# Two transformer blocks on one Trainium2 core: x, the memory tokens, p and the norm weights come feature-major from the host

## The chip, the cores and the metric

The kernel runs on one core of a Trainium2 chip. The metric is the device time of one execution in microseconds. Lower is better.

## The reference

The input x is a float32 sequence of 256 tokens with 2048 features. It goes through a first block of two layers and a second block of one layer. Almost all of the work is products of the 256 tokens with float32 weight matrices; the rest is norms, attention and gates.

```python
# first block, layer 0 (pool) and layer 1 (latent attention)
xn = rms_norm(h, pre_norm[i])
out = pool_mixer(xn, ...) if i == 0 else mla_mixer(xn, ...)
h = h + rms_norm(out, post_norm[i])
gate = sigmoid(rms_norm(h, ple_norm[i]) @ ple_w_gate[i])
h = h + (p[i] @ ple_w_proj[i]) * gate          # p[i]: 256 tokens x 256

# pool_mixer begins with the largest product: 2048 -> 2 * 4096
z = xn @ w_in

# second block: a mixer, cross attention to 256 memory tokens, a feed-forward part
k, v = split(rms_norm(mem, mem_norm) @ w_kv, 2)
```

`rms_norm(x, g)` is x / sqrt(mean(x²) + eps) · g. The weights g are constants of the features; the mean is one number of each token.

## The kernel before, in words

Every engine runs its own hand-written program, and semaphores order them. TensorE contracts over the partitions, so the left operand of a product has to lie feature-major: 128 features on the partitions, 256 tokens along the row, 16 such k-tiles for 2048 features. Tensors that are token-major (`h`, `ptok` for p, `memt` for the memory tokens) are turned by TensorE with an identity matrix, a bank of PSUM for two k-tiles (`to_bank`, L563), and read from the bank by ScalarE and VectorE.

Float32 values are split into a high and a low part: ScalarE writes the high part (`xpose_hi`, L993 or L990: a copy that rounds, times the norm weight, which is one number of each partition), VectorE the remainder (`xpose_lo`, L1375 or L1370). A product is then three matmuls, high·high, low·high, high·low (L598 to L600). The norm's factor 1/rms of each token is multiplied in later, when ScalarE reads the product out of PSUM (`read_out`, L1033).

The weights stream through the core in **units** of 512 KB: two k-tiles by 512 columns. SyncE loads a unit into one of 8 slots of `raw` (L446), ScalarE writes `w_hi` (L968, function `hi`), VectorE writes `w_lo` (L1346, function `lo`), both into rings of 4 slots, and TensorE does 12 matmuls with it. A slot of `raw` is loaded again when its `w_lo` is there; a slot of `w_hi` is written again when TensorE is done with it. I call the units 0, 1, 2, 3 and so on. ScalarE and VectorE are kept three units ahead (`LEAD`): they split units 0 to 2 among the pieces of x, then everything that belongs to the norm of x, and only behind it, in the first loop, unit 3.

At the start SyncE loads the identity, 7 small rows of norm weights, `h` (x, 2 MB, token-major), the band matrix and then the units. GpSimd loads positions, the other norm weights (one row of 128 values on each partition), a mask and p. The norm weights go through TensorE too (`gain_columns`, L649 and L1053). TensorE turns x; at the same time GpSimd squares `h` (L1873), VectorE adds the squares up (L1434, `x_sums`), takes the mean (L1397) and ScalarE the root (`root`, L1028). ScalarE stops at the end of its start part until VectorE has the reciprocal (L1402), since the readings of the loop need it:

```python
root(0)
act.wait_ge(S("rstd0"), 1)
with act.Fori(0, WB) as g, ...        # hi(unit 3) is the first thing in here
```

VectorE does the angles of the rotary embedding (L1412 to L1426) as the first thing of all.

p is turned once for each layer of the first block, shortly before it is used (`xpose(ptok, 2)`): for layer 0 ahead of the product with `yh` and `yl`, for layer 1 right behind attention. The memory tokens are turned piece by piece while their first product runs (`first_chunk`): three pieces of two k-tiles ahead, then one piece after each of the first five units. In that product ScalarE does for each unit a `hi`, a square of `memt` for the norm, and the high part of a piece; VectorE does a `lo` and the low part.

Of the kernel before, what the change touches and what calls it, by code (L numbers as in the profile page):

```python
# [25 lines left out]
D = 2048  # L26
# [42 lines left out]
GAIN_TILES = [  # L69
    [("pre0", 16), ("pre1", 16), ("ple0", 16), ("ple1", 16), ("pool_scale", 32), ("q_norm", 4), ("kv_norm", 4), ("mix", 16)],  # L70
    [("cross", 16), ("ffn", 16), ("mem", 16), ("conv_b", 43)],
    [("conv_w0", 43), ("conv_w1", 43)],
    [("conv_w2", 43)],
]
GAIN = {name: 128 * t + sum(n for _, n in tile[:k]) for t, tile in enumerate(GAIN_TILES) for k, (name, _) in enumerate(tile)}

# [53 lines left out]
class Tally:  # L130


    def __init__(self):
        self.n, self.reg, self.per = {}, None, {}
# [28 lines left out]
def build(nc, a, out):  # L163
# [31 lines left out]
    gain = fixed("gain_columns", [128, 512])  # L195
# [16 lines left out]
    rows = arena("gain_rows", 32768, [128, 4, 128])  # L212
# [16 lines left out]
    ptok = arena("ple_tokens", 116736, [128, 2, 256])  # L229
# [38 lines left out]
    memt = arena("mem_tokens", 32768, [128, 2, D])  # L268
    kvm = arena("mem_kv", KVM, [128, 2, 1024])
# [118 lines left out]
    def heads_done(eng, before):  # L388
# [3 lines left out]
    vectors = {"pre0": a["pre_norm"][0], "pre1": a["pre_norm"][1], "ple0": a["ple_norm"][0], "ple1": a["ple_norm"][1],  # L392
               "pool_scale": a["pool_scale"][0], "q_norm": a["mla_q_norm"][0], "kv_norm": a["mla_kv_norm"][0],
               "mix": a["norm_mix_2"][0], "cross": a["norm_cross_2"][0], "ffn": a["norm_ffn_2"][0],
               "mem": a["mem_norm_2"], "conv_b": a["conv_b_2"][0], "conv_w0": a["conv_w_2"][0, 0],
               "conv_w1": a["conv_w_2"][0, 1], "conv_w2": a["conv_w_2"][0, 2]}

    def load_gains(eng, tiles, sem):

        for n in tiles:  # L400
            at_row = 0
            for name, r in GAIN_TILES[n]:
                eng.dma_start(rows[at_row:at_row + r, n, :], vectors[name].rearrange("(r c) -> r c", c=128)).then_inc(S(sem), 16)
                at_row += r

# [29 lines left out]
    def _(sp):  # L435
# [109 lines left out]
    def _(pe):  # L545
# [96 lines left out]

        pe.wait_ge(S("ident_in"), 16)

        def gain_columns(tiles):
            b = take_bank()
            for n in tiles:
                r = sum(x for _, x in GAIN_TILES[n])
                last = pe.transpose(TB(b)[:, n * 128:n * 128 + r], rows[0:r, n, :], ident[0:r, 0:r])  # L649
            last.then_inc(S("t_full"), 1)  # L650
# [39 lines left out]
        pe.wait_ge(S("ple_in0"), 16)  # L690
        xpose(ptok, 2)
        ready_ple = last_banks(1)
# [120 lines left out]
        attention([MLA], "ukv")  # L813
        pe.wait_ge(S("ple_in1"), 16)
        xpose(ptok, 2)
        ready_ple = last_banks(1)
# [1131 lines left out]
```

## Time and profile before

| | us |
|---|---|
| median of 3 runs | 2696.15 |
| lowest and highest run | 2691.28 and 2705.48 |
| the profiled execution: its own time, from the first to the last instruction (span) | 2694.6 |
| TensorE busy in it | 2621.1 (97%) |
| VectorE busy | 1428.8 (53%) |
| ScalarE busy | 1325.4 (49%) |
| GpSimd busy | 107.4 (4%) |
| mean granted clock of TensorE | 0.989 |
| read from HBM | 443.81 MB |

The profile gives no other time for the profiled execution than its span. The first matmul with weights begins 22.69 us after the start of the span. In a row, the square bracket tells how long the engine was idle before the instruction and who released it. PE is TensorE's matmul, PEld its weight load, DVE is VectorE, ACT is ScalarE, POOL is GpSimd, SP is SyncE.

### The profile page before, as it was taken

How to read it: one execution, taken by the hardware profiler on the slowest of the kernel's cores; microseconds unless marked ns; L12 is line 12 of the kernel's file. 1: busy time of each engine (PE TensorE's matmuls, PEld its weight loads, DVE VectorE, ACT ScalarE, POOL GpSimd, SP SyncE). 2: the span in 40 equal slices, each digit the busy share in tenths (PEclk: the TensorE clock that was granted, in tenths of full speed). 3: DMA queues.
4: the chain of work that ended last, by engine and by line, in shares of the span. 5: the costliest groups of instructions: out<-in, count | busy, mean ns of one | idle time of the engine just before them, and what ended most of it. 6: DMA issues, size and time to landing. Idle time of an engine off the chain costs nothing. (4 is left out here: it accounts for less than half of the span.)

```text
span 2694.6 us, 33963 instructions
## 1 busy us (share of the span) xinstructions
PE 2621.1 (97%) x12046; PEld 2151.4 (80%) x12046; DVE 1428.8 (53%) x1708; ACT 1325.4 (49%) x1792; POOL 107.4 (4%) x158
## 2 busy tenths in 40 slices
PE   7999999999999999999999999999999999999998
PEld 6888888788778987777788887777778888888886
DVE  5444444544655554455545445555556555576554
ACT  4444444544646555455565445345554445454443
POOL 2000000010000001010000001000000000000010
PEclk9999999999999999999999999799999999999999
DMA  7565655556555661365556662035356666655563
GB/s 242 175 182 164 187 168 174 186 184 194 167 168 175 195 183 45 125 211 173 168 173 183 190 192 72 19 126 173 109 178 180 181 184 179 182 161 190 187 200 117
DMA packets 233075, 447.33 MB, mean 166 GB/s; under 512 B 14577, under 2 KB 60065, under 8 KB 232078
## 3 DMA queue, kind: packets, MB, share of 16 engines
q1 hardware_dynamic: 230598, 436.88, 52.5%
q0 software_dynamic: 2352, 9.10, 1.0%
q8 instruction: 63, 1.03, 0.2%
q14 instruction: 38, 0.30, 0.0%
q10 hardware_dynamic: 24, 0.02, 0.0%
HBM read 443.81 MB, written 2.12 MB: 165 GB/s over the span
## 5 line engine op out<-in xcount | busy, mean ns | idle before, releaser
L1346 DVE TENSOR_TENSOR w_lo<-raw,w_hi 128x1024 fp32r<-128x1024 f32 x852 | 1047.2, 1235 | 1017.2 <-ACT w_hi L968 1011.5
L968 ACT ACTIVATE w_hi<-raw 128x1024 fp32r<-128x1024 f32 x852 | 900.1, 1060 | 1066.2 <-PE ps L600 1065.8
L598 PE MATMUL ps<-w_hi,x_hi 128*128 128x512 f32 (+4 forms) x2496 | 979.8, 393 | 20.0 <-DVE x_lo L1375 17.0
L600 PE MATMUL ps<-w_hi,x_lo 128*128 128x512 f32 (+4 forms) x2496 | 970.5, 389 | 0.0
L599 PE MATMUL ps<-w_lo,x_hi 128*128 128x512 f32 (+4 forms) x2496 | 969.1, 388 | 0.0
L598 PEld LDWEIGHTS ps<-w_hi,x_hi 128*128 128x128 f32 x2496 | 471.1, 189 | 126.2 <-issue 19.5
L600 PEld LDWEIGHTS ps<-w_hi,x_lo 128*128 128x128 f32 x2496 | 471.0, 189 | 94.0
L599 PEld LDWEIGHTS ps<-w_lo,x_hi 128*128 128x128 f32 x2496 | 471.4, 189 | 90.6 <-issue 0.2
L598 PE MATMUL ps<-w_hi,ffn_y_hi 128*128 128x512 f32 x344 | 136.6, 397 | 1.8 <-DVE w_lo L1346 1.8
L600 PE MATMUL ps<-w_hi,ffn_y_lo 128*128 128x512 f32 x344 | 136.6, 397 | 0.0
L599 PE MATMUL ps<-w_lo,ffn_y_hi 128*128 128x512 f32 x344 | 136.5, 397 | 0.0
L598 PE MATMUL ps<-w_hi,pool_y_hi 128*128 128x512 f32 x256 | 101.2, 395 | 2.5 <-DVE pool_y_lo L1465 2.5
L599 PE MATMUL ps<-w_lo,pool_y_hi 128*128 128x512 f32 x256 | 101.1, 395 | 0.0
L600 PE MATMUL ps<-w_hi,pool_y_lo 128*128 128x512 f32 x256 | 101.1, 395 | 0.0
L598 PEld LDWEIGHTS ps<-w_hi,ffn_y_hi 128*128 128x128 f32 x344 | 65.3, 190 | 17.2 <-DVE w_lo L1346 2.2
L600 PEld LDWEIGHTS ps<-w_hi,ffn_y_lo 128*128 128x128 f32 x344 | 65.3, 190 | 15.2
L599 PEld LDWEIGHTS ps<-w_lo,ffn_y_hi 128*128 128x128 f32 x344 | 65.2, 190 | 15.1
L1375 DVE SCALAR_TENSOR_TENSOR x_lo<-ps,gain_columns,x_hi 128x256 fp32r<-128x256 f32 x128 | 55.8, 479 | 23.0 <-ACT x_hi L993 18.2
L598 PEld LDWEIGHTS ps<-w_hi,pool_y_hi 128*128 128x128 f32 x256 | 48.3, 189 | 13.8 <-issue 2.7
L993 ACT ACTIVATE x_hi<-ps,gain_columns 128x256 fp32r<-128x256 f32 x128 | 52.7, 467 | 11.9 <-PE ps L563 11.9
L600 PEld LDWEIGHTS ps<-w_hi,pool_y_lo 128*128 128x128 f32 x256 | 48.3, 189 | 11.3
L599 PEld LDWEIGHTS ps<-w_lo,pool_y_hi 128*128 128x128 f32 x256 | 48.3, 189 | 11.1
(281 smaller groups left out, 2000.1 us busy)
## 6 DMA issues: line engine op xcount, KB each, us to landing
raw<-in_w_up SPq DMA_DIRECT2D x160, 512.0 KB, 3.8
raw<-in_pool_w_in SPq DMA_DIRECT2D x128, 512.0 KB, 3.7
raw<-in_w_in SPq DMA_DIRECT2D x96, 480.0 KB, 4.1
raw<-in_w_down SPq DMA_DIRECT2D x76, 512.0 KB, 4.5
raw<-in_pool_w_out SPq DMA_DIRECT2D x64, 512.0 KB, 4.7
raw<-in_ple_w_gate SPq DMA_DIRECT2D x64, 512.0 KB, 4.0
raw<-in_mla_w_in SPq DMA_DIRECT2D x56, 448.0 KB, 4.0
raw<-in_pool_w_group SPq DMA_DIRECT2D x32, 512.0 KB, 4.4
```

The source lines that it names most:

```text
L598: pe.matmul(dst, xhi[:, k, tok], wh, start=k == 0, stop=False)
L599: pe.matmul(dst, xhi[:, k, tok], wl, start=False, stop=False)
L600: last = pe.matmul(dst, xlo[:, k, tok], wh, start=False, stop=k == nkt - 1)
L968: act.activation(w_hi[:, u % RING, :], raw[:, slot, :], ACT.Copy).then_inc(S("w_hi"), 1)
L993: last = act.activation(dst[:, 2 * g + k, :], bank[:, k * 256:k * 256 + 256], ACT.Copy, scale=gain[:, g0 + 2 * g + k:g0 + 2 * g + k + 1])
L1346: dve.tensor_tensor(w_lo[:, u % RING, :], raw[:, u % RAW, :], w_hi[:, u % RING, :].bitcast(F32), ALU.subtract)\
L1375: last = dve.scalar_tensor_tensor(dst[:, 2 * g + k, :], TB(b)[:, k * 256:k * 256 + 256], gain[:, c:c + 1], hi_part[:, 2 * g + k, :].bitcas ...
```

## The change

The host lays out four more inputs: `x_features` and `mem_features` (128 x 16 x 256, feature-major), `p_features` (the same for p, 128 x 2 x 256 for each layer) and `gain_columns` (all norm weights, one column of 128 for each k-tile, 128 x 340). TensorE no longer turns any of them: ScalarE and VectorE read the SBUF tiles `xt`, `memf`, `pfeat` where they read PSUM. The token-major `h` and `memt` are still loaded, for the residual and the sums of squares.

The loads at the start are spread over three queues. SyncE's has the first quarter of `x_features` and then the units. ScalarE's has `gain_columns`, the other three quarters and `h`. GpSimd's has positions, frequencies, the identity, the band matrix, the mask and p. ScalarE and VectorE now do a unit after each of the first three pieces of x, and VectorE does the four sums of squares behind all pieces and the angles behind the reciprocal. The memory tokens are loaded twice, in both layouts, at the place of the one load before.

```diff
+        load(xt[:, 0:4, :], a["x_features"][:, 0:4, :], "x_in0")          # SyncE
-        load(ident, a["c_ident"], "ident_in")
-        load_gains(sp, (0,), "rows_in0")
-        for tt in range(2):
-            load(h[:, tt, :], a["x"][0, tt * 128:(tt + 1) * 128, :], "h_in")
-        load(band.rearrange("p w n -> p (w n)"), a["c_band"], "band_in")
...
+        ready = split_ready("x_split")                                     # TensorE
         pe.wait_ge(S("ident_in"), 16)
-        pe.wait_ge(S("rows_in0"), 16 * len(GAIN_TILES[0]))
-        gain_columns((0,))
-        pe.wait_ge(S("h_in"), 32)
-        xpose(h, KT)
-        ready = last_banks(8)
-        pe.wait_ge(S("rows_in1"), 16 * sum(len(x) for x in GAIN_TILES[1:]))
-        gain_columns((1, 2, 3))
         pe.wait_ge(S("band_in"), 16)
...
-        pe.wait_ge(S("ple_in1"), 16)
-        xpose(ptok, 2)
-        ready_ple = last_banks(1)
+        ready_ple = split_ready("p_split", 1)
         linear(gm)
         layer_end(1, ready_ple)
-        pe.wait_ge(S("mem_in"), 16)
-        first_chunk(memt)
+        chunk(xh, xl, KT, ready=split_ready("mem_split"))
...
+        def split_hi(dst, src, g, g0):                                     # ScalarE
+            for k in range(2 * g, 2 * g + 2):
+                last = act.activation(dst[:, k, :], src[:, k, :], ACT.Copy, scale=gain[:, g0 + k:g0 + k + 1])
+            last.then_inc(S("x_hi"), 1)
+        act.dma_start(gain, a["gain_columns"]).then_inc(S("gains_in"), 16)
+        for n in range(1, 4):
+            act.dma_start(xt[:, 4 * n:4 * n + 4, :], a["x_features"][:, 4 * n:4 * n + 4, :]).then_inc(S(f"x_in{n}"), 16)
+        for tt in range(2):
+            act.dma_start(h[:, tt, :], a["x"][0, tt * 128:(tt + 1) * 128, :]).then_inc(S("h_in"), 16)
+        act.wait_ge(S("gains_in"), 16)
         for g in range(KT // 2):
-            xpose_hi(xh[:, 2 * g:2 * g + 2, :], 2, GAIN["pre0"] + 2 * g)
-            if g in (2, 4, 6):
-                hi(LEAD // 3)
-        gain_columns((1, 2, 3))
+            if g % 2 == 0:
+                act.wait_ge(S(f"x_in{g // 2}"), 16)
+            split_hi(xh, xt, g, GAIN["pre0"])
+            if g < LEAD:
+                hi(1)
         root(0)
...
+        def split_lo(dst, hi_part, src, g, g0, sem):                       # VectorE
+            dve.wait_ge(S("x_hi"), t.at("xh", 1))
+            for k in range(2 * g, 2 * g + 2):
+                last = dve.scalar_tensor_tensor(dst[:, k, :], src[:, k, :], gain[:, g0 + k:g0 + k + 1], hi_part[:, k, :].bitcast(F32),
+                                                ALU.mult, ALU.subtract)
+            last.then_inc(S(sem), 1)
+            t.add("xh")
+        for g in range(KT // 2):
+            split_lo(xl, xh, xt, g, GAIN["pre0"], "x_split")
+            if g < LEAD:
+                lo(1)
+        for c in range(3):
+            x_sums(c)
+        link(x_sums(3))
+        mean(0, D)
+        inverse(0)
...
+        load(ident, a["c_ident"], "ident_in")                              # GpSimd
+        load(band.rearrange("p w n -> p (w n)"), a["c_band"], "band_in")
...
+        load(memf, a["mem_features"], "mem_in")
         load(memt, tokens(a["mem_2"][0]), "mem_in")
```

The order of ScalarE's instructions from its first one on, in the kernel before (names: tile written, then tiles read; `raw` is a weight unit):

```order
L1053 ACT_TABLE_LOAD
L1053 ACTIVATE gain_columns<-ps 128x120
L993 ACTIVATE x_hi<-ps,gain_columns 128x256 x6
L968 ACTIVATE w_hi<-raw 128x1024
L993 ACTIVATE x_hi<-ps,gain_columns 128x256 x4
L968 ACTIVATE w_hi<-raw 128x1024
L993 ACTIVATE x_hi<-ps,gain_columns 128x256 x4
L968 ACTIVATE w_hi<-raw 128x1024
L993 ACTIVATE x_hi<-ps,gain_columns 128x256 x2
```

The same place in the changed kernel:

```order
L1037 DMA gain_columns<-in_gain_columns 128x340
L1039 DMA x_features<-in_x_features 128x1024 x3
L1041 DMA h<-in_x 128x2048 x2
L1034 ACT_TABLE_LOAD
L1034 ACTIVATE x_hi<-x_features,gain_columns 128x256 x2
L948 ACTIVATE w_hi<-raw 128x1024
L1034 ACTIVATE x_hi<-x_features,gain_columns 128x256 x2
L948 ACTIVATE w_hi<-raw 128x1024
L1034 ACTIVATE x_hi<-x_features,gain_columns 128x256 x2
L948 ACTIVATE w_hi<-raw 128x1024
L1034 ACTIVATE x_hi<-x_features,gain_columns 128x256 x10
L1011 ACT_TABLE_LOAD
```

Six transfers now stand ahead of everything, and ten of the sixteen high parts of x (five pieces) stand behind the third unit, where two stood before.

VectorE, from its third unit of weights to the first one of the loop, before:

```order
L1346 TENSOR_TENSOR w_lo<-raw,w_hi 128x1024
L1375 SCALAR_TENSOR_TENSOR x_lo<-ps,gain_columns,x_hi 128x256 x2
L1434 TENSOR_REDUCE square_sums<-x_squares 128x2 x2
L1397 TENSOR_REDUCE mean_square<-square_sums 128x2
L1398 TENSOR_SCALAR mean_square<-mean_square 128x2
L1402 RECIPROCAL rstd<-root 128x2
```

and in the changed kernel:

```order
L1338 TENSOR_TENSOR w_lo<-raw,w_hi 128x1024
L1410 SCALAR_TENSOR_TENSOR x_lo<-x_features,gain_columns,x_hi 128x256 x10
L1419 TENSOR_REDUCE square_sums<-x_squares 128x2 x4
L1392 TENSOR_REDUCE mean_square<-square_sums 128x2
L1393 TENSOR_SCALAR mean_square<-mean_square 128x2
L1397 RECIPROCAL rstd<-root 128x2
L1431 CAST positions_f<-positions 128x2
```

Between unit 2 and the reciprocal VectorE now has ten low parts and four sums in place of two and two, and the angles come between the reciprocal and unit 3.

## Rows read from the trace of the kernel before

**Rows 1.** Page, part 1: engine, busy us (share of the span), instructions.

```profile
PE 2621.1 (97%) x12046; PEld 2151.4 (80%) x12046; DVE 1428.8 (53%) x1708; ACT 1325.4 (49%) x1792; POOL 107.4 (4%) x158
```

**Rows 2.** Timeline, PE, start: start us, us, what [idle before <-releaser].

```profile
12.99 5.73 PE L563 MATMUL ps<-identity,h 128*128 128x128 f32 x28 [5.92 <-DMA h<-in_x]
...
22.69 0.80 PE L598 MATMUL ps<-w_hi,x_hi 128*128 128x512 f32 x1
...
27.98 0.55 PE L598 MATMUL ps<-w_hi,x_hi 128*128 128x512 f32 x1
...
34.73 0.50 PE L598 MATMUL ps<-w_hi,x_hi 128*128 128x512 f32 x1 [0.84 <-DVE w_lo L1346]
```

**Rows 3.** Timeline, ACT, start of the program.

```profile
17.55 1.55 ACT L993 ACTIVATE x_hi<-ps,gain_columns 128x256 fp32r<-128x256 f32 x4
...
31.06 1.28 ACT L968 ACT_TABLE_LOAD   x1 [0.45 <-DVE rstd L1402]
...
32.36 3.90 ACT L968 ACTIVATE w_hi<-raw 128x1024 fp32r<-128x1024 f32 x4
```

**Rows 4.** Timeline, DVE, start of the program.

```profile
5.58 0.20 DVE L1412 CAST positions_f<-positions 128x2 f32<-128x2 int32 x1 [5.58 <-DMA rope_freq<-in_c_freq]
...
8.24 0.19 DVE L1426 TENSOR_SCALAR angle<-angle 128x64 f32<-128x64 f32 x1
...
27.64 2.33 DVE L1434 TENSOR_REDUCE square_sums<-x_squares 128x2 f32<-128x1024 f32 x2
...
30.64 0.17 DVE L1402 RECIPROCAL rstd<-root 128x2 f32<-128x2 f32 x1 [0.27 <-ACT root L1028]
...
33.45 4.63 DVE L1346 TENSOR_TENSOR w_lo<-raw,w_hi 128x1024 fp32r<-128x1024 f32 x4 [2.64 <-ACT w_hi L968]
```

**Rows 5.** Timeline, all engines, start: the transfers of h and the squares.

```profile
0.76 0.39 SPq L454 DMA_DIRECT2D identity<-in_c_ident  x1
...
4.57 0.89 SPq L454 DMA_DIRECT2D h<-in_x  x2
...
13.02 9.01 POOL L1873 TENSOR_TENSOR x_squares<-h 128x512 f32<-128x512 f32 x8 [5.43 <-DMA h<-in_x]
```

**Rows 6.** DMA, 14.5 to 24 us: total of the stretch.

```profile
DMA packets 1921, 3.71 MB, mean 390 GB/s; under 512 B 115, under 2 KB 115, under 8 KB 1921
```

**Rows 7.** DMA, 10.9 to 12.4 us: queue, kind: packets, MB, share.

```profile
q1 hardware_dynamic: 74, 0.43, 69.1%
q0 software_dynamic: 77, 0.20, 33.4%
```

**Rows 8.** Windows: stretch, length, busy (instructions) of PE, PEld, DVE, ACT, POOL; PEclk, DMA share, GB/s.

```profile
1215.00:1300.00 85.00, 84.22 (x363) 67.08 (x362) 47.42 (x55) 42.61 (x59) 0.00 (x0) 1.00 0.53 178
...
1769.00:1772.00 3.00, 0.88 (x5) 0.44 (x5) 3.00 (x9) 1.73 (x3) 0.00 (x0) 1.00 0.57 175
...
1772.00:1775.50 3.50, 3.50 (x12) 2.66 (x11) 2.03 (x3) 0.00 (x0) 0.00 (x0) 0.57 0.22 70
```

**Rows 9.** Timeline, PE, around the transposes of p.

```profile
507.57 0.47 PE L598 MATMUL ps<-w_hi,pool_y_hi 128*128 128x512 f32 x1 [2.50 <-DVE pool_y_lo L1465]
...
1096.54 1.04 PE L563 MATMUL ps<-identity,ple_tokens 128*128 128x128 f32 x4 [0.90 <-DVE mla_gate L1603]
...
1097.37 3.24 PE L563 MATMUL ps<-identity,mla_gate 128*128 128x128 f32 x16
```

**Rows 10.** DMA, 1190 to 1215 us: issues, KB each, median us to landing.

```profile
raw<-in_ple_w_gate SPq DMA_DIRECT2D x7, 512.0 KB, 7.1
mem_tokens<-in_mem POOLq DMA_DIRECT2D x1, 2048.0 KB, 9.8
```

**Rows 11.** Timeline, PE, first product with the memory tokens.

```profile
1301.19 1.91 PE L563 MATMUL ps<-identity,mem_tokens 128*128 128x128 f32 x16
...
1304.45 0.50 PE L598 MATMUL ps<-w_hi,x_hi 128*128 128x512 f32 x1 [1.35 <-DVE x_lo L1375]
...
1321.82 0.47 PE L598 MATMUL ps<-w_hi,x_hi 128*128 128x512 f32 x1 [0.26 <-DVE x_lo L1375]
...
1328.40 0.47 PE L598 MATMUL ps<-w_hi,x_hi 128*128 128x512 f32 x1 [0.26 <-DVE x_lo L1375]
```

More of the change, by code:

```diff
@@ L12 @@
 import math
-from collections import namedtuple
+from collections import defaultdict, namedtuple
 from contextlib import ExitStack, contextmanager
@@ L210, in build @@
     xl = arena("x_lo", 16384, [128, KT, T], F32R)
-    rows = arena("gain_rows", 32768, [128, 4, 128])
+    xt = arena("x_features", 32768, [128, KT, T])
     hsq = arena("x_squares", 71680, [128, 2, D])
@@ L640, in columns, with split_ready @@
                     chunk(xhi, xlo, nkt, width, ready if c == 0 else None)
+        def split_ready(name, before=0):
+            return lambda k: pe.wait_ge(S(name), before + k // 2 + 1) if k % 2 == 0 else None
+        ready = split_ready("x_split")
         pe.wait_ge(S("ident_in"), 16)
[L645 to L650, printed above, removed]
-        pe.wait_ge(S("rows_in0"), 16 * len(GAIN_TILES[0]))
-        gain_columns((0,))
-        pe.wait_ge(S("h_in"), 32)
-        xpose(h, KT)
-        ready = last_banks(8)
-        pe.wait_ge(S("rows_in1"), 16 * sum(len(x) for x in GAIN_TILES[1:]))
-        gain_columns((1, 2, 3))
         pe.wait_ge(S("band_in"), 16)
@@ L1003, in square, with first_chunk @@
             t.add("junk")
-        def first_chunk(g0=None, src=None, slot=None, between=None):
+        def first_chunk(g0=None, src=None, slot=None, between=None, features=None):
             for g in range(KT // 2):
-                xpose_hi(xh[:, 2 * g:2 * g + 2, :], 2, None if g0 is None else g0 + 2 * g)
+                if features is None:
+                    xpose_hi(xh[:, 2 * g:2 * g + 2, :], 2, None if g0 is None else g0 + 2 * g)
+                else:
+                    split_hi(xh, features, g, g0)
                 hi(1)
@@ L1379, in xpose_lo, with first_chunk @@
                 t.add("xh")
-        def first_chunk(g0=None, slot=None, between=None):
+        def first_chunk(g0=None, slot=None, between=None, features=None, sem=None):
             for g in range(KT // 2):
                 k = slice(2 * g, 2 * g + 2)
-                xpose_lo(xl[:, k, :], xh[:, k, :], 2, None if g0 is None else g0 + 2 * g)
+                if features is None:
+                    xpose_lo(xl[:, k, :], xh[:, k, :], 2, None if g0 is None else g0 + 2 * g)
+                else:
+                    split_lo(xl, xh, features, g, g0, sem)
                 lo(1)
@@ L1408, in norm, with x_sums @@
             inverse(slot)
+        def split_lo(dst, hi_part, src, g, g0, sem):
[5 more added lines that the diff above has]
+            t.add("xh")
+        def x_sums(c):
+            dve.wait_ge(S("x_squared"), c + 1)
+            return dve.reduce_sum(sums[:, 0, :, c:c + 1], hsq[:, :, c * 512:(c + 1) * 512], AXX)
+        for g in range(KT // 2):
[7 more added lines that the diff above has]
+        inverse(0)
         dve.wait_ge(S("pos_in"), 32)
@@ L1426, in _ @@
         dve.tensor_scalar(ang, ang, PI, -PI, ALU.min, ALU.max).then_inc(S("rope_reduced"), 1)
-        t.add("bank")
-        dve.wait_ge(S("t_free0"), 2)
-        def x_sums(c):
-            dve.wait_ge(S("x_squared"), c + 1)
-            return dve.reduce_sum(sums[:, 0, :, c:c + 1], hsq[:, :, c * 512:(c + 1) * 512], AXX)
-        for g in range(KT // 2):
-            xpose_lo(xl[:, 2 * g:2 * g + 2, :], xh[:, 2 * g:2 * g + 2, :], 2, GAIN["pre0"] + 2 * g)
-            if g in (2, 4, 6):
-                lo(LEAD // 3)
-            if g in (3, 5):
-                x_sums(g // 2 - 1)
-        t.add("bank")
-        x_sums(2)
-        link(x_sums(3))
-        mean(0, D)
-        inverse(0)
         with dve.Fori(0, WB) as g, t.loop(g, WB, unit=UNITS_POOL, chunk=6, bank=8, xh=4):
@@ L1865, in _ @@
         load(freqs, a["c_freq"].broadcast_to([128, 32]), "pos_in")
-        load_gains(pool, (1, 2, 3), "rows_in1")
+        load(ident, a["c_ident"], "ident_in")
+        load(band.rearrange("p w n -> p (w n)"), a["c_band"], "band_in")
         load(causal, a["c_causal"], "causal_in")
-        load(ptok, tokens(a["p"][0, 0]), "ple_in0")
+        load(pfeat, a["p_features"][0], "ple_in0")
         pool.wait_ge(S("h_in"), 32)
@@ L1876, in _ @@
         products(pool, "proj0")
-        load(ptok, tokens(a["p"][1, 0]), "ple_in1")
+        load(pfeat, a["p_features"][1], "ple_in1")
         def first_mla(j):
```

88 lines of the change are left out of this document (43 added, 45 removed).

## The prediction

> **What bounds the kernel now.** I read the page first: TensorE is busy for 2621.1 of 2694.6 us, every other engine for about half or less [rows 1]. In all it is idle for 73.5 us, and that is the whole stock from which a change off the matmuls can earn. The question for each part of the change is therefore only whether TensorE waits there, and for whom. The timeline of TensorE's first 50 us answers for the start: it waits for x (12.99), turns it, does its first matmul with weights at 22.69, and is then held once more, at 34.73, ahead of unit 3, for VectorE's low part [rows 2]. That second wait is the one that counts. From 34.73 on the weights flow at TensorE's own pace; everything before is a lead that can be lost again. A start that does units 0 to 2 earlier and unit 3 at 34.73 as before wins nothing.
>
> So I followed unit 3 backwards. Its low part begins at 33.45, its high part at 32.36, behind a table load at 31.06 that waited for the reciprocal of the norm [rows 3, 4]. The reciprocal (30.64) needs the root, the mean and the last sum of squares, which ended at 27.64 + 2.33 = 29.97 [rows 4]. The squares are GpSimd's: it began as `h` had landed, at 13.02, and took 9.01 us [rows 5]. From the end of the last sum to unit 3 on TensorE it is 34.73 - 29.97 = 4.76 us, and I keep that piece as it is.
>
> **The start, costed.** Removed are 36 transposes and their reads; they lie ahead of 22.69 and are worth something only if unit 3 moves. Two things have to be there before it now: `h` (for the squares) and unit 2 (since ten high parts of x stand behind it on ScalarE, ten low parts and four sums on VectorE). All queues share the same transfer engines, which give 390 GB/s when full [rows 6]. What is asked for ahead of both: on ScalarE's queue 0.17 MB of norm weights, 1.57 MB of x, 2.10 MB of `h`; on SyncE's 0.52 MB of x and 1.57 MB for units 0 to 2; on GpSimd's 1.26 MB (band 0.79, p 0.26, mask 0.13, identity and small ones 0.08). That is 7.2 MB, 18.5 us at 390 GB/s. To it comes what a transfer takes besides its bytes: `h` was asked for at 4.57 and there at 13.02, 8.45 us for 2.10 MB, which at 390 GB/s are 5.4, so 3.05. The first transfer is issued at 0.76 [rows 5]. The later of the two thus lands at 0.76 + 3.05 + 18.5 = 22.3 us, whichever it is, where before `h` was there at 13.0.
>
> - If unit 2 is the later: its high part takes 1.0 (3.90 for 4), ten high parts of x 3.9 (1.55 for 4) [rows 3], VectorE is half a us behind (my estimate), four sums take 4.7 (2.33 for 2) [rows 4]. The last sum ends at 22.3 + 1.0 + 3.9 + 0.5 + 4.7 = 32.4.
> - If `h` is the later: 9.0 for the squares, 1.2 for the last sum: 32.5.
>
> Either way unit 3 comes 4.76 later, at 37.2, plus the angles: they take 8.24 + 0.19 - 5.58 = 2.85 us [rows 4] and stand between the reciprocal and unit 3's low part, which before began 2.64 after the reciprocal's end (33.45 - 30.81) and was waiting for ScalarE; that adds 0.2. Unit 3 at 37.4 is **2.7 us later than before**. Ends: if GpSimd's 1.26 MB get served behind both, 3.2 us less, unit 3 at 34.2 (-0.5); if the five further units that SyncE asks for (2.62 MB) all get ahead of `h`, 6.7 us more, 44.1 (+9.4).
>
> Arbitration decides between these. Between 10.9 and 12.4 us two queues were served at once: 74 packets of the one and 77 of the other, though 0.43 and 0.20 MB [rows 7]. They take turns by packets, not bytes. `h` is fetched in rows of 8 KB and x in rows of 4 KB, a unit in rows of 2 KB, so ScalarE's queue gets two to four times the bytes of SyncE's, and unit 2 is the later one; `h` behind all units is unlikely. The Trainium skill says the same as a rule (DMA: Bandwidth & Descriptors, "Queues, rings and completion order": each engine round-robins between the rows it has work for, a packet at a time). By it the sum is the first of the two, 37.4; were bytes shared evenly, `h` would end nearer 23, unit 3 near 38. It bears on the chance of the slow rival below.
>
> The clock comes on top. TensorE will have done units 0 to 2 well before 37.4 (unit 2 is split by about 25, and a unit takes 2.8) and idle for some 9 us. After an idle stretch of about 2 us at 1769 the granted clock fell from 1.00 to a mean of 0.57, the lower level being 1.2 GHz, for the next 3.5 us [rows 8]. At the start the first twelve matmuls took from 22.69 to 27.98, 5.29 us [rows 2], where at the full clock (85 us for 363) twelve take 2.8 [rows 8]. Those 2.5 us were paid ahead of the wait at 34.73, where they cost almost nothing; now unit 3 and all behind it pay them. I take **+2.5**; ends 0 and 3.1.
>
> **p.** For layer 0 the transposes are followed by a wait of 2.50 us for `pool_y_lo` [rows 9]: worth 0, and if that cover were gone, 0.6. For layer 1 they stand between attention and the gate's transposes, 1096.54 to 1097.37 [rows 9]: **-0.8**. ScalarE and VectorE do the same two operations from SBUF.
>
> **Memory tokens.** The first product began at 1304.45, released by VectorE's first low part, though TensorE had turned the first pieces from 1301.19 on [rows 11]. ScalarE gets to that piece only behind its reading of the gate, so this start doesn't move; the wait just becomes 3.3 us of pure idling. Of the transposes between units I count what the rows give: five units took 1304.45 to 1321.82, 3.47 each; the two from 1321.82 to 1328.40, with no transposes among them any more, 3.29 each, still waiting 0.26 for `x_lo` [rows 11]. ScalarE and VectorE set 3.29, so five units win 0.9, not the 2.4 that the transposes last. Against it stands the clock: 3.3 us of idling is longer than the stretch at 1769, and 3.5 us at a mean of 0.57 lose 1.5. I take **0** for the sum, ends -0.9 and +1.5. The second load of 2.10 MB at 1197 I cost at nothing: a unit landed in 7.1 us beside the first one, which took 9.8 [rows 10], and a slot is asked for about five units, 14 us, before its use. Without that cover each MB that the units fall behind costs 2 units, 5.6 us.
>
> **The sum.** 2.7 + 2.5 - 0.8 + 0 = +4.4 us: 2699.0 against this execution's 2694.6. Its span lies 1.55 under the median of the runs (2696.15), so I forecast about 2700 for the median. A difference under 0.5%, 13.5 us, is about what a measurement of this kernel can't tell from none: its own runs lie 14 us apart.
>
> **The rivals.**
> - *The whole start moves forward.* The first matmul needs 0.52 MB of x, unit 0 and the band, which with the same again from ScalarE's queue is about 4 MB: 0.76 + 3.05 + 10.3, so 14 us instead of 22.69. If nothing held unit 3, everything would come 8.7 earlier: -8.7 - 0.8 - 0.9 = -10.4, a median of 2686. For it speaks that TensorE's first wait really goes; against it the chain through 9.0 us of squares, which cannot begin before `h`, asked for behind 1.7 MB of its own queue. Chance 0.13.
> - *The favourable order.* Unit 3 at 34.2, no half clock: -0.5 - 0.8 - 0.9 = -2.2, a median of 2694. It needs GpSimd's transfers last, as slow as its mask and p were before. Chance 0.15.
> - *Slower: `h` is starved.* Unit 3 at 44.1, clock 2.5: +9.4 + 2.5 - 0.8 + 0 = +11.1, a median of 2707. It would be told from no change only with `h` later than 31 us. For it speaks that ScalarE's queue is one of three and asks for `h` last; against it the turns by packets. Chance 0.12.
> - The forecast, unit 3 between 36 and 40: a median of 2697 to 2703, chance 0.55. Left for what I don't see: 0.05.
>
> **How the numbers follow.** The predicted time is 2700. The range reaches from 2688 to 2709: below, the favourable order less the scatter of a median of runs that differ by several us; above, the starved `h` with some scatter. Of the first rival most is left out. Faster by over 0.5% (under 2682.7) needs the first rival and luck: 0.06. Slower by over 0.5% (over 2709.6) needs the third and more: 0.07. The rest, 0.87, is no difference that can be told.
>
> **What would show it.** In the changed kernel's timeline: the first matmul with weights well ahead of 22.69 (about 14); then an idle stretch of TensorE of some 9 us ahead of unit 3, put down to `w_lo`; unit 3 at 37.4; GpSimd's squares beginning near 20 instead of 13.0; matmuls 0.43 apart behind the stretch and a granted clock near 0.5 there; the gate's transposes directly behind attention; the first memory product still released by `x_lo` 3.3 us after the last gate matmul, its units 3.3 apart. I am wrong if the squares begin near 13, if unit 3 comes before 34, or if TensorE goes straight on from unit 2.

## The result and the profile after

The changed kernel takes **2732.72 us** (median of 4 runs, 2729.47 to 2737.18) against 2695.16 us (median of 4 runs, 2691.28 to 2705.48) of the kernel before. The ratio is 1.0119, with a 95% interval of [1.0092, 1.0146]; the two medians alone stand at 1.0139. The prediction was 2700, with a range to 2709. It is wrong: the kernel became slower by more than a measurement's scatter. The profiled execution took 2733.06 us, with a span of 2730.9 and a granted clock of 0.982, against a span of 2694.6 and 0.989: 36.3 us to be explained.

The page of the changed kernel, its part 1, answers to [rows 1]:

```profile
span 2730.9 us, 33762 instructions
PE 2634.2 (96%) x11970; PEld 2141.0 (78%) x11970; DVE 1435.0 (53%) x1708; ACT 1326.8 (49%) x1788; POOL 106.7 (4%) x154
```

TensorE does 76 operations fewer and is busy for 13.1 us longer. Its idle time grew from 73.5 to 96.7 us. So there are two questions: what it waits for, and why the same matmuls take longer.

The start first. The timeline of TensorE's first 50 us after the change, which answers to [rows 2]:

```profile
18.06 0.79 PE L595 MATMUL ps<-w_hi,x_hi 128*128 128x512 f32 x1 [18.06 <-DVE w_lo L1338]
...
24.84 0.50 PE L595 MATMUL ps<-w_hi,x_hi 128*128 128x512 f32 x1 [1.68 <-DVE w_lo L1338]
...
29.18 0.50 PE L595 MATMUL ps<-w_hi,x_hi 128*128 128x512 f32 x1 [1.28 <-DVE w_lo L1338]
...
31.85 0.39 PE L597 MATMUL ps<-w_hi,x_lo 128*128 128x512 f32 x1
46.27 0.79 PE L595 MATMUL ps<-w_hi,x_hi 128*128 128x512 f32 x1 [14.03 <-DVE w_lo L1338]
46.86 0.63 PE L596 MATMUL ps<-w_lo,x_hi 128*128 128x512 f32 x1
47.29 0.63 PE L597 MATMUL ps<-w_hi,x_lo 128*128 128x512 f32 x1
```

The first matmul with weights is earlier (18.06 for 22.69), and units 0 to 2 are done by 32. Then TensorE stands still for 14.03 us, and unit 3 comes at 46.27 where it came at 34.73. Behind the wait the matmuls are 0.43 us apart, twice the 0.23 at 25 us. ScalarE in the same stretch (answers to [rows 3]):

```profile
15.69 1.06 ACT L948 ACTIVATE w_hi<-raw 128x1024 fp32r<-128x1024 f32 x1 [7.95 <-DMA raw<-in_pool_w_in]
...
24.77 1.06 ACT L948 ACTIVATE w_hi<-raw 128x1024 fp32r<-128x1024 f32 x1 [0.45 <-DMA raw<-in_pool_w_in]
25.74 4.09 ACT L1034 ACTIVATE x_hi<-x_features,gain_columns 128x256 fp32r<-128x256 f32 x10
...
41.95 0.20 ACT L1011 ACTIVATE root<-mean_square 128x2 f32<-128x2 f32 x1 [10.82 <-DVE mean_square L1393]
```

VectorE (answers to [rows 4]):

```profile
17.92 0.88 DVE L1410 SCALAR_TENSOR_TENSOR x_lo<-x_features,gain_columns,x_hi 128x256 fp32r<-128x256 f32 x2
23.56 1.22 DVE L1338 TENSOR_TENSOR w_lo<-raw,w_hi 128x1024 fp32r<-128x1024 f32 x1 [4.76 <-ACT w_hi L948]
24.70 2.44 DVE L1410 SCALAR_TENSOR_TENSOR x_lo<-x_features,gain_columns,x_hi 128x256 fp32r<-128x256 f32 x2
27.07 2.06 DVE L1338 TENSOR_TENSOR w_lo<-raw,w_hi 128x1024 fp32r<-128x1024 f32 x1
29.05 7.95 DVE L1410 SCALAR_TENSOR_TENSOR x_lo<-x_features,gain_columns,x_hi 128x256 fp32r<-128x256 f32 x10
36.92 4.59 DVE L1419 TENSOR_REDUCE square_sums<-x_squares 128x2 f32<-128x1024 f32 x4
```

And GpSimd (answers to [rows 5]):

```profile
23.73 11.01 POOL L1880 TENSOR_TENSOR x_squares<-h 128x512 f32<-128x512 f32 x8 [18.82 <-DMA h<-in_x]
```

The first square by itself, and VectorE in the window from 29.1 to 34.9:

```profile
23.73 1.95 POOL L1880 TENSOR_TENSOR x_squares<-h 128x512 f32<-128x512 f32 x1 [18.82 <-DMA h<-in_x]
...
29.05 5.97 DVE L1410 SCALAR_TENSOR_TENSOR x_lo<-x_features,gain_columns,x_hi 128x256 fp32r<-128x256 f32 x5
```

A low part of x takes 0.44 us up to 18.80 and 1.2 us from 24.70 to 34.94. Of the ten behind unit 2, five take 5.97 us beside the squares, and the other five, behind the last square (34.74), some 0.4 us each; 0.80 is only their mean. One of the weights takes 1.22 and then 2.06. What changed in between is that GpSimd began to square `h`. The squares take 11.01 instead of 9.01. The four sums stand in VectorE's program behind the low parts, and end at 36.92 + 4.59 = 41.51. From there it is 4.76 us to unit 3, exactly as before.

Behind the start I aligned the two traces by ScalarE's high part of the same unit. So much later it is after the change (my table, from the trace):

| up to | unit | changed kernel | the same with its old addresses (e1, below) |
|---|---|---|---|
| first unit behind the norm | 3 | +11.5 | +11.0 |
| clock back | 7 | +13.2 | +12.7 |
| ahead of p, layer 0 | 131 | +13.8 | +12.4 |
| behind it | 171 | +17.2 | +14.3 |
| ahead of the memory tokens | 414 | +17.7 | +11.8 |
| behind their transposes | 424 | +19.2 | +13.0 |
| ahead of the second attention | 534 | +23.1 | +12.8 |
| behind it | 535 | +34.1 | +23.8 |
| end | 851 | +36.1 | +21.6 |

So 13 us are the start, 11 are one attention late in the program that the change doesn't touch, 3.4 and 1.5 lie where p of layer 0 and the memory tokens were turned, and some 7 are spread over products that the change doesn't touch either. For these the column windows of two stretches with nothing but 480-column matmuls in them, in the kernel before:

```profile
1500.00:1634.00 134.00, 134.00 (x622) 1.00 0.64 192
```

and in the changed kernel (columns: the window, its length, TensorE busy and its matmuls, granted clock, DMA share, GB/s; the second row is a stretch of the second attention):

```profile
1520.00:1657.00 137.00, 137.00 (x624) 1.00 0.62 189
...
1700.00:1757.00 57.00, 55.07 (x186) 0.50 0.11 40
```

A matmul took 134 / 622 = 0.2154 us and takes 137 / 624 = 0.2196, at full clock and without a wait. The attention runs at half clock for 57 us; before it did for 34:

```profile
1687.00:1721.00 34.00, 32.07 (x109) 0.50 0.10 36
```

### The profile page after: what moved, and what is told of

The parts are those of the page before. It is cut to its first block and busy times, and to the rows that moved or that the text cites. A ratio compares the mean times of both kernels' runs of the same rounds, so it can differ in the third digit from the quotient of the medians.

```text
span 2730.9 us, 33762 instructions
## 1 busy us (share of the span) xinstructions
PE 2634.2 (96%) x11970; PEld 2141.0 (78%) x11970; DVE 1435.0 (53%) x1708; ACT 1326.8 (49%) x1788; POOL 106.7 (4%) x154
## 5 line engine op out<-in xcount | busy, mean ns | idle before, releaser
L597 PEld LDWEIGHTS ps<-w_hi,pool_y_lo 128*128 128x128 f32 x256 | 48.7, 190 | 11.9
L596 PEld LDWEIGHTS ps<-w_lo,pool_y_hi 128*128 128x128 f32 x256 | 48.7, 190 | 11.9
L1158 ACT ACTIVATE p_T<-ps 128x384 f32<-128x384 f32 (+1 forms) x40 | 20.1, 502 | 70.8 <-PE ps L763 70.8
L740 PE MATMUL ps<-qk_T 128*128 128x256 f32 (+3 forms) x160 | 50.0, 414 | 1.3 <-ACT qk_T L1165 1.3
```

The lines of the kernel that those rows point to most:

```text
L596: pe.matmul(dst, xhi[:, k, tok], wl, start=False, stop=False)
L597: last = pe.matmul(dst, xlo[:, k, tok], wh, start=False, stop=k == nkt - 1)
L740: last = pe.matmul(dst, QK[s][0:at.d, 0, tok], QK[s][0:at.d, 1, 0:nk], start=at is not FORGETTING and at is not MLA, stop=True)
L1158: act.activation(PTS[s].rearrange("p k n -> p (k n)")[:, 0:at.keys0 + 256], TB(s)[:, 0:at.keys0 + 256], ACT.Copy)\
```

## The experiments

My theory after the result had three parts: the norm weights' tile is 340 columns wide instead of 512, so that all tiles behind it lie 688 bytes (672 after rounding up to 32) lower, and TensorE pays for that in every matmul; the start is later because of `h` and of GpSimd and VectorE hindering each other; the rest is the clock. The rival for the first part was that the extra DMA traffic or the scatter of the clock makes the matmuls slower.

### Addresses

**e1_gain512** is the changed kernel with the old addresses:

```diff
-    gain = fixed("gain_columns", [128, GAIN_COLS])
+    gain = fixed("gain_columns", [128, 512])[:, 0:GAIN_COLS]
```

> The changed kernel with one difference: the tile for the norm weight columns is 512 columns wide again, so that every tile behind it lies at its old address (the change moved them all by 672 bytes, which is 32 bytes off a multiple of 64). Theory A (the addresses cost): matmuls with 480 columns are again 0.2154 us apart in place of 0.2196, the slow drift of about 8 us over the whole span goes, and the time falls to about 2724. If the half-clock stretch in the second attention (58 us long, against 34 before) hangs on the addresses too, about 2713. Theory B (only the start and the clock): the time stays within 3 us of the changed kernel's 2733.

It took 2718.02 us (median of 8), 14.7 less than the changed kernel, with a ratio of 1.0065 [1.0045, 1.0086] to the kernel before. By the table 14.5 us are gone, all outside of the attention. The transfers are the same in both, so they aren't what makes the matmuls slower.

**e2_before_shifted** puts the same displacement (352 bytes; 352 and -672 leave the same remainder by 256) into the kernel before, and nothing else:

```diff
     gain = fixed("gain_columns", [128, 512])
+    fixed("pad", [128, 88])
```

> The kernel before with one difference: an unused tile of 352 bytes behind the norm weight columns, so that the tiles behind it have the changed kernel's addresses up to a multiple of 1024 bytes. Theory A (the addresses cost): 480-column matmuls 0.2196 us apart, 6 to 10 us slower than before, 2702 to 2706; 2713 or more if the long half-clock stretch comes from the addresses. Theory B: no difference, 2693 to 2699.

2716.5 us (median of 4), ratio 1.0075 [1.0058, 1.0091]. Unused bytes alone make it 17 us slower. Not all of that is the matmuls' pace: of the 20.2 us that its trace is longer, 9.4 lie in the second attention, where the half clock lasts 54.6 us instead of 34.1, and 10.8 outside of it. **e0_before_again** is e2's kernel once more; **e4_before_pad32** and **e5_before_pad64** have 32 and 64 unused bytes:

> A second look at the kernel before with shifted addresses, for the granted clock alone. If the length of the half-clock stretch in the second attention is set by the program, it is the same as in the other look within one step of 3.4 us; if it is chance, the two differ by 10 us or more.

> The kernel before with 32 unused bytes behind the norm weight columns. Theory A (TensorE reads its left operand more slowly from rows that begin 32 bytes off a multiple of 64): the same slow pitches as with 352 bytes, 2.675 us a unit in the product with 480 columns (2.630 before) and 2.520 in the last product (2.510 before). Rival (only larger distances, 256 or 512 bytes, matter): the pitches of before.

> The same with 64 unused bytes. Theory A: the pitches of before, 2.630 and 2.510 us. Rival (any shift of the arena costs): 2.675 and 2.520.

They took 2714.11, 2715.68 and, to my surprise, **2666.79 us** (one run each). With 64 bytes the trace is 30 us shorter than that of the kernel before. Two questions followed: is it the tiles' own address or their distance from the weight rings, and after how many bytes does the pattern repeat?

> The kernel before with 64 unused bytes ahead of all of its tiles, so that the raw, w_hi and w_lo rings and the x tiles all lie 64 bytes further, and their distances stay as they are. If only the distance between the weight rings and the tiles matters: nothing changes, 2695 us, with 2.773 us for each 512 KB of weights before pool_out and 2.510 in down. If the address of the tiles itself matters: 2665 us, with 2.730 and 2.472, as with 64 bytes behind the gain columns.

> The kernel before with 128 unused bytes behind the gain columns: the tiles of the arena lie 128 bytes further, the weight rings where they were. If the place within 128 bytes is what matters: 2695 us, with 2.773 us for each 512 KB before pool_out and 2.510 in down, as before. If instead each of the moves tried so far met its own bank pattern over a longer distance: another figure, between 2.73 and 2.79.

> The kernel before with 256 unused bytes behind the gain columns. If the gain grows with the distance from the place of before (0 bytes 2.773, 64 bytes 2.730, 128 bytes 2.703 us for each 512 KB before pool_out): under 2.70. If 128 bytes is one of two halves of a pattern of 256: 2.773, as before. If only a distance that isn't a multiple of some larger power counts: about 2.70.

> The kernel before with 512 unused bytes behind the gain columns. A pattern that repeats within 512 bytes gives 2.773 us before pool_out and 2695 us; one that doesn't gives another figure, at most 2.73.

e12 took 2697.66, e13 2664.85, e15 2696.65 and e16 2699.3 us (one run each; beside e12 and e13 the kernel before took 2706.96 once, beside e15 and e16 2692.86 to 2713.64 in seven runs). TensorE's matmuls in the same 100 us of the second product, at full clock and without a wait, in the kernel before:

```profile
540.00:640.00 100.00, 100.00 (x432) 1.00 0.60 189
```

with the tiles 32 bytes further (e4):

```profile
540.00:640.00 100.00, 100.00 (x430) 1.00 0.59 191
```

64 bytes (e5):

```profile
540.00:640.00 100.00, 100.00 (x439) 1.00 0.58 186
```

128 bytes (e13):

```profile
540.00:640.00 100.00, 100.00 (x443) 1.00 0.60 190
```

and with rings and tiles 64 bytes further (e12):

```profile
540.00:640.00 100.00, 100.00 (x432) 1.00 0.60 193
```

At 256 bytes (e15) the row is that of the kernel before, to the last digit. The reader is to compare the numbers in brackets: the more matmuls, the faster. Over a whole product the differences are clearer. This is the time of a unit (from ScalarE's high parts, in us; my table, from the traces):

| remainder by 256 bytes | runs | second product | 480 columns | last product |
|---|---|---|---|---|
| 0 | before, e1, e12, e15, e16 | 2.772 to 2.773 | 2.676 | 2.513 |
| 32 | e4 | 2.784 | 2.711 | 2.524 |
| 64 | e5 | 2.729 | 2.688 | 2.476 |
| 96 | changed, e2, e0 | 2.784 | 2.720 | 2.524 |
| 128 | e13 | 2.702 | 2.678 | 2.452 |

Rings and tiles moved together change nothing, so it is the distance between what lies ahead of the padding (the weight rings) and what lies behind it (the left operands) that counts, not the address. In these runs it counts by its remainder by 256: 256 and 512 bytes give the kernel before again, 32 and 96 are slower, 64 and 128 faster. It isn't alike in all stages: the 480-column product wins nothing at 64 or 128 bytes. That the two operands of the matmul itself get in each other's way is likely but not shown, since the distance from the left operands to `raw`, which transfers write and ScalarE and VectorE read, changed by the same bytes. Against these two engines speaks that in the window of the kernel before the matmuls follow each other 0.232 us apart (my count from the trace) whether VectorE, ScalarE or neither of the two is at work.

The scatter of the clock is not the cause. The kernel before ran 61 times beside the experiments, and its time follows its mean granted clock: 2689 us at 0.992, 2693 to 2699 at 0.990, 2704 to 2707 at 0.986, 2713 to 2714 at 0.983. Against its runs of like clock e4 (0.986) is some 10 us slower and e2 (0.985 to 0.987) 10 to 13; e5 (0.990) is some 28 and e13 (0.985) some 43 us faster; e12, e15 and e16 (0.988 and 0.989) lie among them.

**e11_changed_64** is the changed kernel with a gain tile of 528 columns, 64 bytes beyond the old place:

> The changed kernel itself, its norm weight tile 528 columns wide, so that what lies behind is 64 bytes beyond its old place, in place of 672 bytes ahead of it. If the addresses are worth what the kernel before shows (28 us), 2718 - 28 = 2690, under the kernel before; if the change in itself loses more than that, 2700 or above.

2692.03 us (median of 10), ratio 0.9953 [0.9928, 0.9978]: the change plus 188 columns of nothing is faster than the kernel before. Its unit 3 is still 12.4 us late; at unit 416 it is 1.6 late. But its distance has the remainder of e5, and in the window of above it shows the pace of 32 or 96 bytes:

```profile
540.00:640.00 100.00, 100.00 (x431) 1.00 0.61 200
```

Through the whole second product a unit takes 2.784 us here, not 2.729, while in the last one it takes 2.476 as in e5; e10 below, with the same remainder, has 2.729 again. And e0 and e2, one and the same kernel, take 2.538 and 2.556 us a unit in the product that follows the first gate. So the remainder sets the pace in most products and launches, but something else that no run here isolates can undo it.

### The start

**e8_squares_held** (on e1) lets GpSimd begin only when the last low part of x is there, **e9_transfers_spaced** (on e1) spreads the requests at the start: the later pieces of x are asked for behind a unit each, then `h`, and band, mask and p come behind the squares.

```diff
+        pool.wait_ge(S("x_split"), 8)                                      # e8, ahead of the squares
...
+        load_x(1)                                                          # e9, ScalarE
...
+                if g < 2:
+                    load_x(g + 2)                                          # behind hi(1)
+                else:
+                    for tt in range(2):
+                        act.dma_start(h[:, tt, :], ...)
```

> The changed kernel with the old addresses, GpSimd's squares held until all low parts of x are there. Theory (GpSimd and VectorE slow each other when both work from SBUF): the ten low parts behind unit 2 take 0.44 us each in place of 0.80 and the squares 9.0 us in all in place of 11.0; the low parts end near 30.5, the squares at 39.5, the last sum at 40.8, unit 3 at 45.5. Rival (VectorE is slow because it reads SBUF in place of PSUM): 0.80 stays, the low parts end near 37, unit 3 is near 52.

> The changed kernel with the old addresses and only the order of the transfers altered: ScalarE asks for the last quarters of x and for h one after the other as units 0 to 2 land, GpSimd for band, mask and p behind the squares. ScalarE and VectorE still turn to the norm ahead of unit 3. Theory (the transfers of the other two queues crowd out the units): unit 0 at 11.4 in place of 15.2, unit 2 near 15 in place of 24, h near 26; then squares and sums to 38.5, unit 3 near 43: 3 us earlier than in the changed kernel though h itself is 3 us later. Rival (h decides all alone): unit 3 at 46 plus 3.

e8 took 2719.91, e9 2715.0 us (one run each). The timeline of e8, three engines:

```profile
27.37 4.04 DVE L1410 SCALAR_TENSOR_TENSOR x_lo<-x_features,gain_columns,x_hi 128x256 fp32r<-128x256 f32 x10
...
45.60 0.80 PE L595 MATMUL ps<-w_hi,x_hi 128*128 128x512 f32 x1 [13.33 <-DVE w_lo L1338]
...
31.57 8.03 POOL L1881 TENSOR_TENSOR x_squares<-h 128x512 f32<-128x512 f32 x8 [26.66 <-DVE x_lo L1410]
```

Kept apart, ten low parts take 4.04 instead of 7.95 us and the squares 8.03 instead of 11.01. Each engine does slow the other down; and since VectorE reads x from SBUF in both, that alone isn't what made it slow. But unit 3 comes at 45.60, where e1's comes at 45.72: done one after the other they need as long. In the changed kernel the first square began 0.17 us after a low part of the weights, took 1.95 us instead of 1.0, and from the end of that low part (24.78) the two engines went in turn, one operation each, to the last square (34.74): seven low parts of x, one of the weights and eight squares. By the times without the other that is 2.83 + 1.22 + 8.03 = 12.1 us; it took 10.0. The Trainium skill (SBUF — State Buffer, "Who interferes with whom") says that a VectorE instruction with two inputs in SBUF and a GpSimd instruction that reads SBUF exclude each other fully. By that rule it would be 12.1; the trace agrees in the strict turns, but the two operations of a pair overlap by about a quarter of a us, 2 us in all.

In e9 the order of the transfers alone is different (the same two rows):

```profile
13.76 0.80 PE L595 MATMUL ps<-w_hi,x_hi 128*128 128x512 f32 x1 [13.76 <-DVE w_lo L1343]
...
40.79 0.79 PE L595 MATMUL ps<-w_hi,x_hi 128*128 128x512 f32 x1 [16.58 <-DVE w_lo L1343]
...
26.77 8.02 POOL L1882 TENSOR_TENSOR x_squares<-h 128x512 f32<-128x512 f32 x8 [23.45 <-DMA h<-in_x]
```

ScalarE's high part of unit 0 begins 4.3 us earlier than in the changed kernel (11.39), the squares 3.0 later, and unit 3 still 4.9 us earlier than in e1, since no low part lies beside the squares or ahead of the sums any more.

### p and the memory tokens, and the clock

**e3_p_mem_only** is the kernel before with the part of the change that is about p and the memory tokens; **e6_p_mem_warm** adds 14 and 16 matmuls of the identity on itself where the transposes were, into a bank that is overwritten later.

```diff
+        for _ in range(14):                                                # e6, ahead of y's first unit
+            pe.matmul(MM(0, 1)[:, 0:128], ident, ident, start=True, stop=True)
...
-            chunk(xh, xl, KT, ready=split_ready("mem_split"))
+            chunk(xh, xl, KT, ready=split_ready("mem_split"), warm=16)     # 16 of them ahead of the memory product
```

> The kernel before with the change of p and of the memory tokens alone: start, norm weights and addresses as before. If the start costs 13 us and the addresses 8 to 20, what is left for this part is: -0.8 for the transposes of p in layer 1, +2.5 where TensorE idles 3.0 us ahead of the product with y at a clock that falls, +1.5 at the memory tokens: about +3, 2698. Rival: the removed transposes are a plain gain of 3 to 4 us, 2692.

> The kernel before with p and the memory tokens feature-major, and with matmuls of the identity with itself, whose results nobody reads, in TensorE's two idle stretches: 14 ahead of the product with y, 16 ahead of the first memory product. Theory (the removed transposes had kept the clock up): the half-clock stretches of 3.4 us at 522 and at 1321 go, and the time falls by 3 to 4 us against the same kernel without them (2705), to about 2701, with the scatter of the second attention's half-clock stretch on top. Rival (those stretches come whatever TensorE does in the gap): no change, 2705.

e3 took 2705.37 us (median of 10), ratio 1.0017 [0.9997, 1.0036]; e6 2700.47 (10), ratio 0.9996 [0.9970, 1.0022]. The intervals overlap; that the dummy matmuls win is not shown by the times. What they do is seen in the traces. In the timeline of the changed kernel TensorE waits for `pool_y_lo` as in [rows 9], but longer, and comes back at half clock; the last row is its first matmul of the memory tokens, which answers to [rows 11]:

```profile
521.60 0.77 PE L595 MATMUL ps<-w_hi,pool_y_hi 128*128 128x512 f32 x1 [2.99 <-DVE pool_y_lo L1465]
522.17 0.63 PE L596 MATMUL ps<-w_lo,pool_y_hi 128*128 128x512 f32 x1
522.59 0.63 PE L597 MATMUL ps<-w_hi,pool_y_lo 128*128 128x512 f32 x1
...
1322.26 0.48 PE L595 MATMUL ps<-w_hi,x_hi 128*128 128x512 f32 x1 [3.25 <-DVE x_lo L1410]
```

Its granted clock is 0.52 from 521 to 528 and 0.57 from 1323 to 1327 (windows of the same view as above); in the kernel before and in e6 it is 1.00 in both places. From unit 131 to 171 e3 loses 1.7 us against the kernel before and e6 0.2; from 414 to 424 e3 loses 1.2 and e6 nothing. That is the price of the half clock.

At the memory tokens the transposes had been holding it off: the clock fell there in all six profiles of kernels without transposes and dummies, and in none of the nine with transposes or the four with dummies. Ahead of the product with y the record is less clean. The clock fell in the same six and in none of the four, but also in two of the nine that have the transposes, e12 and e2. This is e2, with the same 2.50 us of waiting as in [rows 9] (first a row of the timeline, then one of the windows):

```profile
511.19 0.47 PE L599 MATMUL ps<-w_hi,pool_y_hi 128*128 128x512 f32 x1 [2.50 <-DVE pool_y_lo L1466]
...
511.90:515.30 3.40, 3.40 (x9) 0.50 0.03 5
```

It loses 1.8 us from unit 131 to 171, as much as e3. In e0, the same kernel with the same wait, the clock stayed at 1.00. So the transposes make the fall rarer there, and whether it comes differs between executions.

### Together

**e7_start_freed** takes e1, e9 and e6 together and has the first pass of the pool mixer's loop written out ahead of the loop, so that ScalarE and VectorE do units 3 to 10 ahead of the norm. **e10_freed_64** and **e14_freed_128** are e7 with its tiles 64 and 128 bytes further (528 and 544 columns).

```diff
+        def pool_turn(g, off, first=False):                                # ScalarE
...
+                s = chunk(8)
+                if first and c == 0:
+                    root(0)
+                    act.wait_ge(S("rstd0"), 1)
...
+        pool_turn(0, 0, first=True)
+        with act.Fori(0, WB - 1) as g, ...:
```

> The changed kernel with the old addresses, those unused matmuls, and another start: ScalarE asks for the second quarter of x at once, for the others one by one as the first units land, and for h behind unit 2; GpSimd asks for band, mask and p behind the squares; ScalarE and VectorE do units 3 to 10 before they turn to the norm. Theory (the start was lost to transfers that crowd out the units, and to unit 3 waiting for the norm): unit 0 lands near 7 us, the first matmul is near 10, no stretch over 2 us without matmuls up to 60 us, h lands near 22, and the time is some 13 us under the kernel before: about 2686. If the units are slow for another reason, the first matmul stays near 18 and the gain is under 5 us.

> The kernel with the freed start (2691 in its own rounds), and the tiles behind the norm weight columns 64 bytes further on. By the pitches of the kernel before with 64 bytes (2.730 us a unit in the product with y in place of 2.773, 2.472 in the last in place of 2.510) the time falls by some 28 us, to about 2663, 37 under the kernel before. If the 64 bytes worked only with the old start, it stays at 2691.

> The version with the freed start and its tiles 128 bytes further (544 columns for the gain in place of 528). If distance alone does it, the pitches are those of the tiles at 128 bytes (2.703 before pool_out, 2.448 in down), and the time lies 5 to 15 us under the 2665 us of 64 bytes less. If the start and the second attention's clock outweigh it: 2660 to 2670 us.

| | median us (runs) | ratio to the kernel before |
|---|---|---|
| e7_start_freed | 2691.03 (10) | 0.9958 [0.9934, 0.9982] |
| e10_freed_64 | 2665.38 (6) | 0.9859 [0.9828, 0.9890] |
| e14_freed_128 | 2655.84 (4) | **0.9807 [0.9749, 0.9865]** |

e7 took 5 us more than expected. In it TensorE's first matmul is at 13.79, not near 10, with no wait of over 1 us before 40, and from unit 3 on the units are 9.6 to 11.9 us earlier than before, up to the second attention. Behind it they are 1.0 earlier: that attention is at half clock for 58.0 us in this trace too.

## Why the prediction was wrong

**Not in the sum at all: the addresses.** The step "what bounds the kernel" took the matmuls' duration for given and looked for gains and losses in TensorE's 73.5 idle us alone. The change makes one tile narrower, and all behind it move. e1 against the changed kernel: 14.7 us by the medians, and by the traces none of it in the second attention; e2 against the kernel before: 17.5, of which by the traces some 9 are the second attention's clock, so that 8 (e4) to 11 us (e2) are left. With the start this is the largest term, and it is shown from both sides; its exact size isn't.

**"Unit 3 at 37.4, 2.7 us later": it came at 46.27, 11.5 later.** The mechanism (x's low parts and `h` gate the norm, the norm gates unit 3) was right, its sizes were not. The first matmul came at 18.06 and not near 14, since unit 0 was there only at 15.69, and the wait ahead of unit 3 was 14.03 us and not some 9. Unit 2's high part began at 24.77, where the sum had 22.3, and `h` was there at 23.73: 2.5 and 1.4 us. The larger error is "ten high parts 3.9, VectorE half a us behind": the ten low parts, five of them beside the squares, took 7.95, and unit 2's own 2.06. So the last sum ended at 41.51 instead of 32.4: 2.5 for the landing; 3.2 until VectorE got to the ten, at 29.05, though unit 2's high part had ended at 25.83; 3.5 for the ten (7.95 for 3.9 + 0.5); and -0.1 for the sums. I had costed VectorE and GpSimd each as if alone, from rows in which VectorE read x from PSUM. And I had taken the later of two branches, squares or low parts, where they share something and so add up: e8 shows that undoing the overlap wins nothing. The 4.76 us behind the sums held to the hundredth. The turns by packets don't explain the rest: e9 shows that the requests' order was worth 4.9 us, which the sum had as nothing.

**"Clock +2.5" at the start.** The half clock came where forecast, with unit 3, and cost 1.7 us up to unit 7. Right in the mechanism, 0.8 too much in size.

**p, layer 0, "worth 0, and if that cover were gone, 0.6": +1.7 to +3.4.** The wait for `pool_y_lo` did hide the time of the transposes, but without them TensorE idled for 2.99 us in one piece and the clock fell, for 6.8 us in the changed kernel and 3.4 in e1 and e3. Such a fall was already in [rows 8]; I counted with it at the start and the memory tokens, not here. e2 pays 1.8 with its transposes in place; so a part of this term is the luck that the fall was absent from the profile of the kernel before. **p, layer 1, -0.8:** between units 346 and 348 the changed kernel wins 1.7 and e1 1.8, but there the 3.4 us of half clock that the kernel before has at 1096.7 are gone too. e0, e2 and e4 keep the transposes and haven't that half clock either; they win 1.1. That leaves some 0.7 for the transposes: right. **Memory tokens, 0 with ends -0.9 and +1.5:** +1.5 in the changed kernel, +1.2 in e1 and e3 (units 414 to 424), near the upper end; the 3.3 us of idling (3.25) and the clock of 0.57 are as forecast.

**Not in the sum: the second attention, +11.0.** The half clock there lasts 58.0 us instead of 34.1. It isn't specific to the change: it is 54.6 in e2 and e8, 41.0 in e3, 30.7 in e5 and e15, 27.3 in e6, 58.0 in e7 and e13, which is the kernel before but for 128 bytes. The kernel before varies too, from 2689 us at a granted clock of 0.992 to 2714 at 0.983; and a run of e1 at a clock of 0.992 took 2700.93 where the others took 2713 to 2721. Yet it isn't mere scatter either: the four runs of the changed kernel have clocks of 0.979 to 0.983, the 61 of the kernel before 0.983 to 0.992, so the low clock came each time. What decides how long the clock stays low in this attention stays open. I could not tie it to when the attention begins, nor to what is ahead of it.

The rivals: h was starved only by 1.4 us, the start as a whole didn't move forward, and the slow rival's 2707 named neither the contention nor the addresses. Had the addresses been left alone, the time would have been 2718, still outside of the range.

## What to carry to other kernels

When an edit changes a tile's size, ask what it moves, and time a version with the old addresses beside it: here 128 unused bytes gave more (2664.85 against 2706.96 us, one run each) than the whole edit cost, and trying 64 and 128 bytes of padding between the weight rings and the left operands is the cheapest experiment there is. Small fillers between products (transposes) may be what keeps TensorE's clock up; before taking them away, look at how long the idle stretch becomes in one piece. And when work moves so that VectorE and GpSimd read SBUF at once, cost them as one engine, not as two: it came within 2 us of the 12.1 measured one by one.

## What the runs showed of the hardware

- The distance in SBUF between the weight rings and the left operands changes the pace of the matmuls, and in these runs by its remainder by 256 bytes. In 100 us there were 432 matmuls of 512 columns at the distance of before, 430 with 32 bytes more, 439 with 64, 443 with 128, 432 with 256; with both operands moved by 64 it stayed at 432. One run (e11) had the remainder 64 and 431. Against runs of like clock the whole kernel was 10 to 13 us slower at 32 and 96 bytes, some 28 faster at 64 and 43 at 128.
- VectorE's low part of x (two of its inputs in SBUF) took 1.2 instead of 0.4 us, that of the weights 2.06 instead of 1.22, beside GpSimd's squares, which took 11.01 instead of 8.03 us. The two engines went in turn, an operation each.
- Idle stretches of 2.99 and 3.25 us were followed by a granted clock of 0.52 over 7 us and 0.57 over 4 us; with 14 and 16 small matmuls in them it stayed at 1.00. After one of 2.50 us it fell to 0.50 in e2 and stayed at 1.00 in e0, the same kernel.
